# Linear scan of the even mixer: a head's tiles two and three projected in its own first two steps, the next head's projections two steps later

## The reference, cut to what matters

```python
def forget_gate(f_raw, lb):
    z = f_raw.astype(jnp.float32)
    log_f = jnp.logaddexp(jnp.log(lb), jnp.log1p(-lb) + jax.nn.log_sigmoid(z))
    k = (1.0 - lb) * jax.nn.sigmoid(-z)
    return k, log_f
...
    def step(S, inp):
        qc, kc, gc, vc = inp
        b = jnp.cumsum(gc, axis=2)
...
        scores = jnp.einsum("bhtd,bhtsd,bhsd->bhts", qc, decay, kc)
        o = jnp.einsum("bhts,bhsv->bhtv", scores, vc) + jnp.einsum("bhtd,bhdv->bhtv", qc * jnp.exp(b), S)
...
    def readout(o, g):
        return (rms_norm(o, out_norm_w).reshape(B_, n, B_V_W) * jax.nn.silu(g)).astype(g.dtype)
```

## Time and profile before

| | |
|---|---|
| median of 3 runs | 2387.15 us (2385.52 to 2388.26) |
| profiled execution | 2387.81 us, span 2386.0 us, mean granted TensorE clock 0.981 |
| TensorE products busy | 2286.1 us, 96% of the span |
| VectorE, ScalarE, GpSimd busy | 1444.7, 1138.0, 80.2 us (61, 48, 3%) |

### The profile page before, as it was taken

How to read it: one execution, slowest core, us unless ns; L and a number is a source line. 1 busy time by engine, 2 the same in 40 slices (tenths; PEclk the granted TensorE clock), 3 DMA queues, 4 the chain that set the end, 5 groups by cost and what they waited for, 6 DMA issues and landing times. The chain is left out here.

```text
span 2386.0 us, 37881 instructions
## 1 busy us (share of the span) xinstructions
PE 2286.1 (96%) x14434; PEld 1861.1 (78%) x14434; DVE 1444.7 (61%) x2402; ACT 1138.0 (48%) x1960; POOL 80.2 (3%) x117
## 2 busy tenths in 40 slices
PE   8999999999999989999999997999999989989998
PEld 7887878788888868787568886788888768867886
DVE  6665457657665447666566666474554654447887
ACT  4443455444443455434367665343443444445654
POOL 0000000000000000000002222000000000000000
PEclk9999999999999999999999999999999979999999
DMA  9887316775887425873121110244333433305662
GB/s 271 267 261 210 111 54 214 253 257 165 251 261 230 114 84 167 261 250 111 65 70 46 46 63 19 71 124 120 117 105 113 144 92 85 98 11 158 194 193 89
DMA packets 389939, 346.84 MB, mean 145 GB/s; under 512 B 24388, under 2 KB 353464, under 8 KB 389304
## 3 DMA queue, kind: packets, MB, share of 16 engines
q1 hardware_dynamic: 380029, 294.62, 41.7%
q10 hardware_dynamic: 9787, 50.52, 5.4%
HBM read 344.05 MB, written 1.05 MB: 145 GB/s over the span
## 5 line engine op out<-in xcount | busy, mean ns | idle before, releaser
L716 PE MATMUL ps<-x_hi_lo,gu_hi 128*128 128x512 f32 x1680 | 423.7, 394 | 2.3 <-DVE gu_sum L914 2.3
L716 PEld LDWEIGHTS ps<-x_hi_lo,gu_hi 128*128 128x128 f32 x1680 | 305.7, 188 | 81.5 <-issue 19.7
L914 DVE TENSOR_REDUCE gu_sum<-ps 128x256 f32<-128x512 f32 x220 | 150.3, 689 | 242.9 <-PE ps L718 242.8
L817 ACT ACTIVATE gu_hi<-w_gu 128x1024 fp32r<-128x1024 f32 x220 | 229.3, 1054 | 117.1 <-DVE gu_sum L914 50.9
L897 DVE TENSOR_TENSOR gu_lo<-w_gu,gu_hi 128x1024 fp32r<-128x1024 f32 x220 | 260.8, 1219 | 15.9 <-ACT gu_hi L817 15.7
L718 PEld LDWEIGHTS ps<-x_hi_lo,gu_lo 128*128 128x128 f32 x1680 | 228.8, 190 | 16.8
L718 PE MATMUL ps<-x_hi_lo,gu_lo 128*128 128x256 f32 x1680 | 233.8, 282 | 0.0
L745 PE MATMUL ps<-dn_hi,h_hi 128*128 128x512 f32 x440 | 173.4, 394 | 2.1 <-DVE h_lo L941 2.1
L745 PE MATMUL ps<-dn_lo,h_hi 128*128 128x512 f32 x440 | 172.5, 392 | 0.0
L745 PE MATMUL ps<-dn_hi,h_lo 128*128 128x512 f32 x440 | 171.3, 389 | 0.0
L833 ACT ACTIVATE silu<-gu_sum 128x256 f32<-128x256 f32 x88 | 36.7, 417 | 260.7 <-DVE gu_sum L914 260.0
(11 more groups left out here) (508 smaller groups left out, 4787.1 us busy)
## 6 DMA issues: line engine op xcount, KB each, us to landing
w_gu<-in_ffn_w_up SPq DMA_DIRECT2D x176, 512.0 KB, 6.3
w_dn<-in_ffn_w_down SPq DMA_DIRECT2D x132, 512.0 KB, 3.5
w_mod<-in_w_mod ACTq DMA_DIRECT2D x64, 768.0 KB, 6.9
w_gu<-in_ffn_w_gate SPq DMA_DIRECT2D x88, 512.0 KB, 5.1
odd_w<-in_odd_w_qkv SPq DMA_DIRECT2D x24, 512.0 KB, 5.2
w_gu<-in_ffn_w_down SPq DMA_DIRECT2D x11, 1024.0 KB, 4.8
hgrn_w<-in_even_w_in SPq DMA_DIRECT2D x20, 512.0 KB, 3.9
wo<-in_w_out SPq DMA_DIRECT2D x2, 4096.0 KB, 12.8
```

The lines of the kernel that those rows point to most:

```text
L716: pe.matmul(gu(a), gu_hi[n][:, a, f, :], x_both[:, f, :, :], start=(f == 0), stop=False, skip_group_check=True)
L817: act.activation(gu_hi[n][:, a, :, :], wgu[n][:, a, :, :], ACT.Copy).then_inc(s["w_hi"], 1)
L914: dve.reduce_sum(c[n][:, a, :], gu(a).rearrange("p h t -> p t h"), AX.X).then_inc(s["c_ready"], 1)
```

## The change

VG23 of a head is projected in the head's own steps 0 and 1 (half-slots 8 and 9). The half-slots 0 to 5 of the next head move to steps 2 to 7, 6 stands before `turn_decays` and 7 behind the first cross scores. All that feeds or follows the half-slots moves two steps with them: the splits of the weights, `keep_keys`, `soft_exp`, and to step 7 `keep_queries`, `soft_ln` and VectorE's `decays`. `keep_values` of VG23 stands in ScalarE's step 2, `keep_values` of VG01 at the boundary. The Silu of the queries stays at the boundary; that of the gates runs at the boundary behind the head's own scan, and for the last head in its step 3. The first head uses bank 3 like the others, and the constants of the sums are copied by VectorE, not by ScalarE.

```diff
--- before.py
+++ after.py
@@ -2848,7 +2848,7 @@
 
             def proj_bank(h, c):
 
-                return k.ps[:, (4, 5, 6, 3, 7)[c] if h == 0 else 3, :]
+                return k.ps[:, 3, :]
 
             def gate_and_value(h):
 
@@ -2910,7 +2910,7 @@
                     c, half = SLOTS[n]
                     bank = proj_bank(h, c)
                     pe.wait_ge(s["w_lo"], 5 * h + (c if c < VG01 else V) + 1)
-                    if half == 0 and h:
+                    if half == 0:
                         pe.wait_ge(s["proj_used"], 5 * h + c)
                     if c < VG01:
                         for f in range(4 * half, 4 * half + 4):
@@ -2959,8 +2959,6 @@
                     elif i:
                         pe.wait_ge(s["masked"], unit(i - 1, NU - 1))
                         pe.wait_ge(s["x_used"], 2 * i)
-                    else:
-                        pe.wait_ge(s["proj_used"], 5)
                     for n in range(NSUB):
                         for i4 in range(P // SUB):
                             b4 = slice(i4 * SUB, (i4 + 1) * SUB)
@@ -2979,8 +2977,10 @@
                     if u == 0:
                         if i:
                             pe.wait_ge(s["y_used"], i)
+                        pe.wait_ge(s["proj_used"], 5 * i + 4)
+                        pe.matmul(k.ps[:, O, :], k.zero[:, :], k.x_T[:, 0, :], start=True, stop=False, skip_group_check=True)
+                    if u == 2:
                         pe.wait_ge(s["proj_used"], 5 * i + 5)
-                        pe.matmul(k.ps[:, O, :], k.zero[:, :], k.x_T[:, 0, :], start=True, stop=False, skip_group_check=True)
                     pe.wait_ge(s["ends_ready"], unit(i, u))
                     pe.matmul(k.ps[:, O, tt * P:(tt + 1) * P], pr[:, u % 2, :], values_of(i, tt), start=False, stop=False,
                               skip_group_check=True).then_inc(s["pv_done"], 1)
@@ -3026,18 +3026,19 @@
                         last = pe.transpose(k.ps[:, O, tt * P:(tt + 1) * P], y[:, tt, :], k.ident[:, :])
                     last.then_inc(s["y_turned"], 1)
 
-                for n in range(2 * EARLY, 9):
+                for n in range(2 * EARLY, 8):
                     slot(0, n)
                 turn_decays(0)
-                slot(0, 9)
                 sums(0, 0)
                 for i in range(BH):
                     more = i < LAST
                     for u in range(NU):
                         if u:
                             sums(i, u)
-                        if more:
-                            slot(i + 1, u)
+                        if u < 2:
+                            slot(i, 8 + u)
+                        elif more:
+                            slot(i + 1, u - 2)
                         if u == 2 and i:
                             turn_out(i - 1)
                         if u >= 1:
@@ -3045,12 +3046,12 @@
                         if u >= 3:
                             values(i, u - 3)
                     if more:
+                        slot(i + 1, 6)
                         turn_decays(i + 1)
-                        slot(i + 1, 8)
                         scores(i, NU - 1)
                         values(i, NU - 3)
                         cross_scores(i, 0)
-                        slot(i + 1, 9)
+                        slot(i + 1, 7)
                         values(i, NU - 2)
                         cross_values(i, 0)
                         cross_scores(i, 1)
@@ -3118,11 +3119,14 @@
                         act.wait_ge(s["k_pre"], 2 * h + d + 1)
                         act.activation(keys_of(h, d), keys_of(h, d), ACT.Exp, scale=-1.0).then_inc(s["k_ready"], 1)
 
-                def silus(h):
+                def silu_queries(h):
+                    act.wait_ge(s["proj_used"], 5 * h + Q + 1)
+                    flat_q = q[:, h % 2, :, :].rearrange("p t d -> p (t d)")
+                    act.activation(flat_q, flat_q, ACT.Silu).then_inc(s["silu_q"], 1)
+
+                def silu_gates(h):
                     act.wait_ge(s["proj_used"], 5 * h + 5)
-                    flat_q = q[:, h % 2, :, :].rearrange("p t d -> p (t d)")
-                    act.activation(flat_q, flat_q, ACT.Silu).then_inc(s["silu_done"], 1)
-                    act.activation(gates_of(h), gates_of(h), ACT.Silu).then_inc(s["silu_done"], 1)
+                    act.activation(gates_of(h), gates_of(h), ACT.Silu).then_inc(s["silu_g"], 1)
 
                 def decays_hi(h):
                     for d in range(2):
@@ -3174,48 +3178,43 @@
                     act.activation(ab[:, d, :], z[:, d, :], ACT.Abs).then_inc(s["abs_ready"], 1)
                 soft_exp(0)
                 soft_ln(0)
-                for d in range(2):
-                    last = act.activation(cum[:, d, :, :].rearrange("p b n -> p (b n)"), m.e[:, d, :], ACT.Copy)
-                last.then_inc(s["cum_ready"], 1)
                 keys(0)
+                decays_hi(0)
                 keep_values(0, VG01)
-                decays_hi(0)
+                silu_queries(0)
                 split(1, K0)
-                keep_values(0, VG23)
-                silus(0)
                 for i in range(BH):
                     more = i < LAST
                     for u in range(NU):
                         decay_tile(i, u)
                         if u >= 2:
                             score_ends(i, u - 2)
-                        if u == 0:
+                        if u == 0 and i:
+                            norm(i - 1)
+                        if u == 2:
+                            keep_values(i, VG23)
                             if more:
                                 split(i + 1, K1)
                             if i:
-                                norm(i - 1)
-                        if u == 1 and more:
-                            keep_keys(i + 1, 0)
-                        if u == 2:
-                            if more:
-                                split(i + 1, Q)
-                            if i:
                                 keep_output(i - 1)
                         if u == 3 and more:
+                            keep_keys(i + 1, 0)
+                        if u == 3 and not more:
+                            silu_gates(i)
+                        if u == 4 and more:
+                            split(i + 1, Q)
+                        if u == 5 and more:
                             split(i + 1, G)
                             keep_keys(i + 1, 1)
-                        if u == 4 and more:
+                        if u == 6 and more:
                             split(i + 1, V)
                             soft_exp(i + 1)
-                        if u == 5 and more:
+                        if u == 7 and more:
                             keep_queries(i + 1)
-                        if u == 6 and more:
                             soft_ln(i + 1)
-                        if u == 7 and more:
-                            keep_values(i + 1, VG01)
                             keys(i + 1)
-                        if u in (1, 3, 4, 5) and not more:
-                            out_weights((1, 3, 4, 5).index(u))
+                        if 3 <= u < 7 and not more:
+                            out_weights(u - 3)
                         if u >= 6 and not more:
                             for n in (2 * (u - 6), 2 * (u - 6) + 1):
                                 out_inputs(n)
@@ -3224,8 +3223,9 @@
                         score_ends(i, NU - 2)
                         score_ends(i, NU - 1)
                         keep_cross(i, 0)
-                        keep_values(i + 1, VG23)
-                        silus(i + 1)
+                        keep_values(i + 1, VG01)
+                        silu_queries(i + 1)
+                        silu_gates(i)
                         keep_cross(i, 1)
                     if i + 2 <= LAST:
                         split(i + 2, K0)
@@ -3287,11 +3287,13 @@
                         flat_d = lambda a: a[:, d, :, :].rearrange("p t d -> p (t d)")
                         dve.tensor_tensor(flat_d(g_lo), k.ps[:, d, :], flat_d(g_hi).bitcast(F32), ALU.subtract).then_inc(s["g_lo"], 1)
 
-                def queries_and_gates(h):
-                    dve.wait_ge(s["silu_done"], 2 * h + 1)
+                def queries(h):
+                    dve.wait_ge(s["silu_q"], h + 1)
                     q_all = q[:, h % 2, :, :].rearrange("p t d -> p (t d)")
                     dve.tensor_scalar(q_all, q_all, HGRN_SCALE, None, ALU.mult).then_inc(s["q_ready"], 1)
-                    dve.wait_ge(s["silu_done"], 2 * h + 2)
+
+                def gates(h):
+                    dve.wait_ge(s["silu_g"], h + 1)
                     dve.tensor_tensor(gates_of(h), gates_of(h), gain[:, :].unsqueeze(1).broadcast_to([P, TILES, P]), ALU.mult).then_inc(s["gate_ready"], 1)
 
                 def products(i, u):
@@ -3346,27 +3348,32 @@
                                                         ALU.mult, ALU.mult)
```

(20 more changed lines are left out.)

2 lines of the change are left out of this document (1 added, 1 removed).

## The result

| | before | after |
|---|---|---|
| median | 2386.34 us (2385.52 to 2388.26, 4 runs) | 2398.43 us (2394.60 to 2401.13, 4 runs) |
| profiled execution | 2387.81 us, span 2386.0 | 2401.13 us, span 2399.3 |
| mean granted clock | 0.981 | 0.979 |

The ratio is 1.0049 (95% interval 1.0037 to 1.0061): the change makes the kernel slower by about 12 us (8.8 to 14.6 by the interval), half a percent. The forecast was 2397.8. One execution of the kernel before, in the session of the last four experiments, took 7878.55 us and is in no ratio; all others lie in the ranges given.

What follows compares the result with a forecast made beforehand. TensorE's queue was taken to bound the first three heads, latencies between engines the fourth. Terms -2.8 + 5.1 + 4.5 - 0.3 - 1.5 + 1.1 = +6.1, with the clock +10.6, gave 2397.8 us; range 2389.5 to 2402.5.

Steps and rivals of the forecast that it cites:

- The new wait in step 2: Step 2, TensorE waits for ScalarE's copy of values and gates: stall 2.9 us; heads 2 and 3 together +5.1.
- Rival (d): Step 2's copy is out before TensorE wants the bank: -2.2, with the boundary hidden -6.7, 2380.5; chance 0.06.
- the meant gain: Two half-slots leave the time before each head and fall into the last head's idle time: at best 5.8 us.
- The boundary: From step 7's sums, cross scores at 13.9 to 14.0 us instead of 12.38: +1.5, three times, +4.5.
- Rival (c): The boundary hides its delay: 4.5 less and no further clock loss, +1.6, 2388.8, no difference; chance 0.12.
- The start: First head: sums of step 3 at 1279.75 against 1282.56, -2.8.
- the walk: Step-by-step timing of the scan at the 2.4 GHz level throughout; summed without lost clock to +6.1.
- The last head: Lead at step 3 eaten by the gates' Silu, its table loads and VectorE's full queue: +1.1, between 0 and 2.
- Rival (e): A table switch costs more than its row, say 2 x 1.28 in the last head: 2395.8 to 2400.4; chance 0.05.
- The clock: Six waits before dense work, half costing 1.5 each: +4.5; separately -1.5 credited for the first boundary's earlier loss.
- rival (b): The clock falls behind every new wait: +15, 2402.2; chance 0.13.
- rival (a): The timing of the scan without lost clock: +6.1, 2393.2; chance 0.26.

Runs made afterwards that it cites:

- last four experiments: Four of the follow-up kernels, run on another chip than the first four, with the kernel before at 2387.30 us (2385.38 to 2389.14, 15 runs).
- early_copy: Changed kernel with ScalarE's copy of values and gates of tiles two and three put ahead of step 2's exponential: 2388.38 us, ratio to before 1.0007.
- both: Changed kernel with the edits of `early_copy` and `boundary` together, nothing else: 2381.26 us, ratio to before 0.9976.
- boundary: Changed kernel with step 7's scores ahead of turning the decays, and their mask ahead of cross operands and low parts: 2390.71 us, ratio to before 1.0020.
- fill: Changed kernel with products of zeros in TensorE's waits before step 2's half-slot and the first cross scores, nothing moved: 2392.27 us, ratio to before 1.0026.

## Why the prediction was right, and what was off in it

**The new wait in step 2 (right).** Forecast was 2.45 us in the first head and 2.9 in the others; the trace has 2.29, 3.05 and 3.06, released by ScalarE's copy. `early_copy` shows the cause: with the copy two places ahead the wait is gone and 10 us with it. Rival (d) set the point from which the meant gain would appear, a copy finished 1.18 us after step 2's sums start. `early_copy` and `both` are kernels beyond it, and `both` came out 5.1 below the kernel before, at 2381.26 where that rival, with the boundary's delay gone too, had 2380.5.

**The boundary (right, 0.1 to 0.2 too large).** Cross scores at 13.9 to 14.0 us behind step 7's sums were forecast, 13.77 came; the wait before turning is 0.48 and not 0.9, the one before the cross scores 2.50 and not 2.7. `boundary`, which puts the scores ahead of the turning and the mask ahead of the cross operands and low parts, has 12.24. The prediction laid the delay on VectorE's queue ("only then the mask of step 7"); the trace lets the low parts hold the mask up by 0.66 us only, and has the scores of step 7 themselves late, behind the turning. Rival (c), that the delay is hidden, is out.

**The start.** Step 3 of the first head came 1.3 us earlier, not 2.8. Its half-slot took 4.43 us where 2.92 is the full clock; the 1.5 missing are clock. The rest of the walk holds in its times (sums of step 0, 1, 2 at 9.0, 14.6 and 19.4 us behind the first product; forecast 9.3, 14.4 and 19.4), but partly by luck: the first sums, behind a wait of 1.69 us, ran at a clock of 0.53 in this execution, and step 0 took 5.56 us where `boundary`, `fill` and `both` have 4.99. VectorE's two casts, without a row before, took 1.43 us together, hidden as assumed.

**The last head (+0.5, forecast +1.1).** Its products of step 5 began 26.7 us after its first sums, forecast 26.9. The head is 0.9 late up to its first cross scores (34.92 us behind its first sums, before 34.02) and 0.5 at its second (42.88, before 42.39); 0.4 comes back between the two. Rival (e), a switch that costs more than its row, is out by the timeline of ScalarE in the changed kernel's last head:

```profile
1470.56 1.28 ACT L3129 ACT_TABLE_LOAD   x1
1471.85 0.63 ACT L3129 ACTIVATE hgrn_vg<-hgrn_vg 128x512 f32<-128x512 f32 x1
1472.39 1.04 ACT L3168 ACTIVATE hgrn_h_hi<-h_T 128x1024 fp32r<-128x1024 f32 x1
1473.45 1.28 ACT L3142 ACT_TABLE_LOAD   x1
1474.74 1.13 ACT L3142 ACTIVATE hgrn_e<-ps 128x1152 f32<-128x1152 f32 x1
```

Each load starts 0.02 us behind the work before it (1472.39 + 1.04 = 1473.43) and is followed 0.01 us behind its end. The drain of some 1.38 us that the Trainium skill (ScalarE: Activation LUTs, What ACT_TABLE_LOAD costs) adds does not appear in these two switches. What does appear is that the exponential of step 4 is no earlier for all the lead, 21.7 us behind the head's first sums (1453.05 to 1474.74; before 21.45, forecast 21.8), and that TensorE waits 1.64 us for it.

**The clock (the mis-sized term).** The step that failed in size is "if half of them cost 1.5 each: +4.5". The 1.5 is right (1.5 to 1.6 each), the half is not: in the profiled execution all six waits lost it, and the first boundary lost it again, so that the credit of 1.5 there was real but eaten. That is the case of rival (b) for this execution. The median lies lower: `fill` puts the clock at 6.2 (2398.43 - 2392.27), about four waits of six. The same run measures the walk without clock at +5.9 (2392.27 - 2386.38), where rival (a) had +6.1. So the forecast's 10.65 above the median before stands against 12.1, and in the medians nearly all of the difference is the clock term (4.5 against 6.2).

That the total came out so close is in part luck. In the profiles the two terms are off in opposite ways: the walk without clock is +4.2 and not +6.1, the clock 9.9 and not 4.5. And the forecast stood on a median before of 2387.15, which one more run brought to 2386.34.

One of its grounds was misread. The prediction has 0.50 "behind" the wait of 2.6 in the last head and cites the stretch 1450.00 to 1454.00. The clock was down before that wait, which runs from 1450.81 to 1453.40. The table of stretches of the kernel before:

```profile
1446.40:1448.40 2.00, 0.62 (x41) 0.44 (x26) 0.03 (x1) 1.99 (x2) 0.00 (x0) 1.00 0.03 8
1448.40:1450.00 1.60, 1.16 (x5) 1.16 (x6) 1.18 (x2) 1.34 (x2) 1.11 (x1) 0.77 0.00 0
1450.00:1451.00 1.00, 0.82 (x3) 0.31 (x1) 1.00 (x2) 0.15 (x1) 0.00 (x0) 0.50 0.00 0
```

It fell behind the wait of 1.82 us that ends at 1448.85. So all that the kernel before showed of lost clock in the scan came behind waits of 1.8 to 1.9 us.

**The period.** "61.5 us from the second head's first sums to the third's" was said of the walk without lost clock. The profile after shows 64.36, `fill` 61.18.

**Where the gain would have been.** The prediction looked for it in the last head. In `both` the first product to the last head's first sums takes 182.15 us (1251.70 to 1433.85) and 187.36 before, that is 5.2 less, and the last head 0.5 more. Two half-slots of the last head are no longer in front of it, 5.9, as the prediction worked out; where that shows first is the start of the scan: head 2 begins 66.3 us behind the first product instead of 72.2, since the order of all heads slides by two half-slots.

## What to carry to other kernels

When one buffer is handed round between producers, the place of the copy that empties it in the *other* engine's queue decides: put it ahead of the next instruction that waits for the producer itself, and behind nothing that depends on it. When a block of work is moved in an ordered queue, list what stood between its result and the next critical consumer on every engine (here the turning ahead of the scores on TensorE, and the cross operands and low parts ahead of the mask on VectorE) and restore that order. Price a new wait of TensorE before dense work with the clock, not with the wait alone, and test the two apart by filling the wait with products of zeros.

## What the runs showed of the hardware that was not expected

**Whether a wait costs clock is not set by its length alone.** TensorE's clock is at its level of 2.4 GHz in these stretches before the wait, and at 1.2 GHz for a while behind some. Counted over the profiles of the ten kernels, at the waits of the first three heads in step 2 and before the cross scores (lost: the same work behind the wait takes longer than at the full clock, as 8.9 us for 7.33):

| wait, us | waits | of them with the clock lost behind |
|---|---|---|
| 0.33 to 0.84 (filled) | 12 | 0 |
| 1.88 to 1.90 | 14 | 7 |
| 2.29 | 2 | 1 |
| 2.50 | 6 | 6 |
| 3.05 to 3.42 | 5 | 5 |

`boundary` and `both` have the same order around the same wait of 1.9 us and lost it at none and at all three of their boundaries. Shorter ones can cost too: of the eight kernels with a wait of 1.69 or 1.70 us before the first sums of the scan, only the changed one lost clock there. What decides at these lengths is not shown. Nearly every loss was 1.5 to 1.6 us; at the second boundary of `early_copy` it was 2.65 (1370.55 to 1380.54 is 9.99 us, 7.33 at the full clock), with the clock at 0.50 over the first 4 us.

**The spread of a kernel may be in part this; that is not shown.** After has 6.5 us between its fastest and slowest of four runs. But the kernel before has 5.0 in 31 runs, and `fill`, with the waits filled, still 4.8 in ten.

**Products of zeros are cheap cover.** Ten of 128x128 (two records each) took 2.39 us, 0.24 each, and in `fill` the clock stayed at 1.00 from the second head to the fourth (1317.80 to 1440.10).
